# Order of the expert passes, time of the routing ranks, and order of the products in a streaming-encoder kernel

## The reference

```python
def swiglu(x, w1, w3, w2):
    return (jax.nn.silu(x @ w1) * (x @ w3)) @ w2

def moe_swiglu(h, router_w, w1, w3, w2):
    logits = (xf @ router_w).astype(jnp.float32)
    top_val, top_idx = lax.top_k(logits, TOP_K)
    gates = jax.nn.softmax(top_val, axis=-1)
    ...
    y = lax.map(expert_block, (buf_tok.reshape(n_blocks, EXPERT_BLOCK), block_exp))
    y = y.reshape(P, D) * buf_g[:, None].astype(y.dtype)
    out = jax.ops.segment_sum(y, buf_tok, num_segments=N + 1)[:N]
```

## Time and profile before

| | |
|---|---|
| median of 3 runs | 1400.2 us (1400.18 to 1401.83) |
| profiled execution, its own time | 1399.86 us |
| its span | 1398.1 us |
| TensorE busy | 1295.9 us (93%), mean granted clock 0.956 |
| VectorE busy | 920.8 us (66%) |
| ScalarE busy | 743.0 us (53%) |
| HBM read | 472.46 MB, 339 GB/s over the span |

### The profile page before, as it was taken

The page is one execution under the profiler, slowest core; times in us unless marked ns, Lnnn a source line. Parts: engine busy times, 40 slices in busy tenths (PEclk is TensorE's granted clock), DMA queues, the critical chain, the costliest instruction groups (busy, mean ns, idle before and its releaser), DMA issues. The chain is left out here.

```text
span 1398.1 us, 20800 instructions
## 1 busy us (share of the span) xinstructions
PE 1295.9 (93%) x7888; PEld 942.5 (67%) x7888; DVE 920.8 (66%) x1547; ACT 743.0 (53%) x1279; POOL 10.5 (1%) x45
## 2 busy tenths in 40 slices
PE   7999999999999999999779999999869997699985
PEld 5875899999888988786138888887216652067420
DVE  3788898887885669996049999998017730077201
ACT  4656554444563669893049998996016730067100
POOL 0000000000000200000000000000000000000000
PEclk9999999999999999999979999999969999799896
DMA  8986668879665449899999999999999979999796
GB/s 322 378 299 235 247 243 297 320 268 358 242 235 188 156 158 378 338 366 354 420 413 415 404 413 413 407 417 356 419 418 411 420 277 420 418 405 419 266 418 256
DMA packets 130146, 474.92 MB, mean 340 GB/s; under 512 B 9437, under 2 KB 11626, under 8 KB 107514
## 3 DMA queue, kind: packets, MB, share of 16 engines
q1 hardware_dynamic: 128672, 472.28, 87.0%
q10 hardware_dynamic: 1370, 1.25, 0.3%
HBM read 472.46 MB, written 1.05 MB: 339 GB/s over the span
## 5 line engine op out<-in xcount | busy, mean ns | idle before, releaser
L2315 ACT ACTIVATE hi_first<-ring 128x512 fp32r<-128x512 f32 x166 | 103.3, 632 | 43.0 <-DMA ring<-in_moe_w 30.1
L3139 DVE TENSOR_TENSOR lo_first<-ring,hi_first 128x512 fp32r<-128x512 f32 x166 | 108.7, 691 | 15.6 <-ACT hi_first L2315 15.3
L3139 DVE TENSOR_TENSOR lo_third<-ring,hi_third 128x512 fp32r<-128x512 f32 x168 | 109.9, 691 | 12.8 <-ACT hi_third L2315 12.0
L2315 ACT ACTIVATE hi_third<-ring 128x512 fp32r<-128x512 f32 x168 | 103.9, 632 | 19.4 <-PE bank L1748 12.8
L2315 ACT ACTIVATE hi_second<-ring 128x512 fp32r<-128x512 f32 x166 | 103.0, 633 | 18.9 <-PE bank L1748 12.9
L3139 DVE TENSOR_TENSOR lo_second<-ring,hi_second 128x512 fp32r<-128x512 f32 x166 | 108.6, 691 | 4.9 <-ACT hi_second L2315 4.3
L2556 DVE SCALAR_TENSOR_TENSOR ada_acc<-ring,c_act,ada_acc 128x512 f32<-128x512 f32 x140 | 105.1, 751 | 3.9
L1827 PE MATMUL bank<-ring,work 128*32 128x512 f32 x344 | 67.8, 874 | 37.3 <-DMA ring<-in_moe_w 37.3
L1833 PE MATMUL bank<-ring,work 128*32 128x512 f32 x672 | 90.1, 605 | 7.2 <-DMA ring<-in_moe_w 7.2
L1282 PE MATMUL bank<-hg_hi,w_hi 128*128 128x256 f32 x336 | 95.5, 284 | 0.4 <-DVE w_lo L2791 0.4
L1284 PE MATMUL bank<-hg_hi,w_lo 128*128 128x256 f32 x336 | 95.1, 283 | 0.0
(11 more groups left out here) (560 smaller groups left out, 3336.0 us busy)
## 6 DMA issues: line engine op xcount, KB each, us to landing
ring<-in_moe_w SPq DMA_DIRECT2D x216, 1024.0 KB, 18.6
ring<-in_ada_w SPq DMA_DIRECT2D x24, 2048.0 KB, 12.1
ring<-in_moe_w SPq DMA_DIRECT2D x48, 768.0 KB, 11.2
ring<-in_ffn_w SPq DMA_DIRECT2D x15, 2048.0 KB, 9.4
beside_x<-in_moe_w SPq DMA_DIRECT2D x18, 1024.0 KB, 17.7
beside_out<-in_moe_w SPq DMA_DIRECT2D x18, 1024.0 KB, 17.6
beside_w<-in_moe_w SPq DMA_DIRECT2D x18, 1024.0 KB, 17.0
beside_lo<-in_moe_w SPq DMA_DIRECT2D x18, 1024.0 KB, 19.6
```

Source lines behind the costliest of these rows:

```text
L2315: A(hi_piece(Q), raw_piece(SPLITS[r], q, j), ACT.Copy).then_inc(hi_done, 1)
L3139: v.tensor_tensor(lo_piece(Q), raw_piece(SPLITS[r], q, j), hi_piece(Q).bitcast(F32), ALU.subtract).then_inc(lo_done, 1)
```

## The change

The order becomes A head, B, A tail, C head, B, C tail, A head, B, A tail, A, B. Three light passes lie inside the first, the wide and the next ordinary pass; the wide pass is second. Each of these light passes has its own gather, in the head of its host at pieces 35 and 38. In a hosting ordinary pass `slots_turned` moves from piece 20 to 54. In the first pass the ranks move from piece 28 to 4 (the fifth piece), the gain vector from 36 to 12 and to banks 2 and 3, the tokens' places from 33 to 14, the light pass's table to 20, and the next passes' tables stay at 60. SP waits for the ranks after slot 11. The low-part product of each part comes last, in the dense stage and in the expert passes, and the wait for the low part stands before it; the other two products wait for the high part alone. Branches for overflow passes go six deep instead of four. Waits on earlier results are left out where there is no earlier result.

```diff
-BASE = "ABAABCBB"
+BASE = "ABCBABAB"
-PLACES = (NE - 1, 3, 1, 2, 4, 0, 5, 6)
+PLACES = (NE - 1, 3, 0, 4, 1, 5, 2, 6)
-MIDS = {5: 6}
+MIDS = {0: 1, 2: 3, 4: 5}
...
-    PT_AT = {"A": g_last["w3", 0] + 5, "C": g_last["w3", 2] + 5}
+    PT_AT = {"A": g_last["w3", 0] + 5, "host": PPC * CUT + 6, "C": g_last["w3", 2] + 5}
...
-    GAIN_AT = g_last["w3", 1] + 5
-    PLACES_AT = GAIN_AT - 8
-    OVER_AT = GAIN_AT + 12
-    DISPATCH_AT = {"A": OVER_AT + 12, "C": XPT_AT + 3}
+    PLACES_AT = 4
+    GATES_AT = 8
+    GAIN_AT = 12
+    TOKENS_AT = 14
+    MID_DISPATCH_AT = 20
+    DISPATCH_AT = {"A": g_last["w3", 1] + 29, "C": XPT_AT + 3}
...
-    GROUPS = [(0,), (1, 2), (3,), (4, 5), (6,), (7,)] + [(NE + o,) for o in range(OVER)]
-    group_in = {0: 1, 2: 2, 3: 3, 5: 5}
-    mid_group_in = {5: 4}
-    dispatched_in = {0: (1, 2), 2: (3,), 3: (4, 5, 6), 5: (7,)}
+    GROUPS = [(0,), (1,), (2,), (3,), (4,), (5,), (6,), (7,)] + [(NE + o,) for o in range(OVER)]
+    group_in = {0: 2, 2: 4, 4: 6, 6: 7}
+    mid_group_in = {0: 1, 2: 3, 4: 5}
+    dispatched_in = {0: (2, 3), 2: (4, 5), 4: (6,), 6: (7,)}
...
-                if m == 0 and i >= PER - NE + 1:
+                if m == 0 and (i == CUT - 1 or i >= PER - NE + 2):
                     j = len(ids)
                     sp.wait_ge(s_places, 1)
...
-                pe.wait_ge(lo_done, q + 1)
+                pe.wait_ge(hi_done, q + 1)
                 whi, wlo = split_tile(w_hi, q), split_tile(w_lo, q)
+                out = psum[4 + g % 2][:, o:o + S]
                 for k in range(KT):
-                    out = psum[4 + g % 2][:, o:o + S]
                     mm(out, whi[:, k, :], hg_hi[:, k, :], start=(k == 0), stop=False)
                     mm(out, whi[:, k, :], hg_lo[:, k, :], start=False, stop=False)
+                pe.wait_ge(lo_done, q + 1)
+                for k in range(KT):
                     last = mm(out, wlo[:, k, :], hg_hi[:, k, :], start=False, stop=(k == KT - 1))
...
-                    pe.wait_ge(lo_done, piece_no(m, q, 0) + 1)
...
-                        pe.wait_ge(lo_done, Q + 1)
+                        pe.wait_ge(hi_done, Q + 1)
...
                         mm(out[:, :], xhi, whi, start=first, stop=False)
-                        mm(out[:, :], xhi, wlo, start=False, stop=False)
-                        mm(out[:, :], xlo, whi, start=False, stop=end).then_inc(w_free, 1)
+                        mm(out[:, :], xlo, whi, start=False, stop=False)
+                        pe.wait_ge(lo_done, Q + 1)
+                        mm(out[:, :], xhi, wlo, start=False, stop=end).then_inc(w_free, 1)
...
-                    if q == PT_AT[kind]:
+                    if q == PT_AT[role(m)]:
                         slots_turned(m)
...
-                            last = mm(psum[6 + k // 4][:, (k % 4) * P:(k % 4 + 1) * P], ones[:], diag[:, k, :],
+                            last = mm(psum[2 + k // 4][:, (k % 4) * P:(k % 4 + 1) * P], ones[:], diag[:, k, :],
...
-                    if q == 8 and m == 0:
+                    if q == GATES_AT and m == 0:
                         first_gates()
...
-                    if q == PLACES_AT + 5 and m == 0:
+                    if q == TOKENS_AT and m == 0:
                         places_of_tokens()
+                    if q == MID_DISPATCH_AT and m == 0:
+                        dispatch(MIDS[m])
...
                         with pe.If(more[3] == 2):
                             overflow(3)
+                            with pe.If(more[4] == 2):
+                                overflow(4)
+                                with pe.If(more[5] == 2):
+                                    overflow(5)
```

More of the change, by code:

```diff
@@ L287, in build @@
         plan = sb("plan", [P, 2, NE])
-        with ExitStack() as of_ranks:
-            ranks_of = of_ranks.enter_context(nc.sbuf_tensor("ranks_of", [P, TT, NE * NE], F32))
+        ranks_of = sb("ranks_of", [P, TT, NE * NE])
         members_of, earlier_e = [ranks_of[:, tt, :] for tt in range(TT)]
-        mid_places = sb("mid_places", [P, TT, HALF], F32R)
+        mid_places = sb("mid_places", [P, TT, XT], F32R)
         rt = sb("rt", [P, 12, TT * NE])
@@ L303, in build @@
         h_hi = sb("h_hi", [P, TT, D], F32R)
-        Pm = sb("Pm", [P, TT, P + 2 * XT], F32R)
+        Pm = sb("Pm", [P, TT, P + XT], F32R)
         QK_FILLS = (0, 2, 1, 3, 4, 6, 5, 7)
@@ L686, in outs_before, with role @@
             return turn_no(m) - (m in MIDS) if m < NE else m - 1
+        def role(m):
+            return "host" if m in MIDS and KINDS[m] == "A" else KINDS[m]
         def down_bank(m):
@@ L1324, in ffn_out @@
                         mm(out, whi[:, 0, ms], xlo, start=False, stop=False, skip_group_check=True)
+                    pe.wait_ge(lo_done, q + 1)
+                    for m in range(KT):
+                        out = psum[m // 2][:, (m % 2) * S:(m % 2 + 1) * S]
+                        ms = slice(m * P, (m + 1) * P)
                         last = mm(out, wlo[:, 0, ms], xhi, start=False, stop=end, skip_group_check=True)
@@ L1708, in expert @@
                             pe.wait_ge(s_ea, chunk_no(m, c))
-                            if kind == "A" and c == 1:
+                            if kind == "A" and c == (2 if role(m) == "host" else 1):
                                 pe.wait_ge(s_gge, turn_no(m) + 1)
@@ L1714, in expert @@
                                 pe.wait_ge(s_scb, 4 * out_no(MIDS[m]) + 2)
-                            if c == 2 and m == 0:
+                        else:
+                            if c == 0 and m == 0:
                                 pe.wait_ge(s_g2e, 1)
-                        else:
-                            if c == 0 and m:
+                            if c == 0 and outs_before(m):
                                 pe.wait_ge(s_scb, 4 * outs_before(m))
@@ L1761, in expert @@
                             pe.wait_ge(s_hdl, chunk_no(m, turn))
-                        elif m:
+                        elif outs_before(m):
                             pe.wait_ge(s_scb, 4 * outs_before(m))
@@ L1811, in light @@
                         else:
-                            pe.wait_ge(s_scb, 4 * outs_before(m))
+                            if outs_before(m):
+                                pe.wait_ge(s_scb, 4 * outs_before(m))
                             pe.wait_ge(s_hdh, chunk_no(m, 0) + 1)
@@ L2426, in expert @@
                             A(hidx[:, turn % 2, 0:js, :], turned[:, :, 0:2 * XT], ACT.Silu).then_inc(s_xs, 1)
-                    if q == PT_AT[kind] + 1:
+                    if q == PT_AT[role(m)] + 1:
                         take_slots(m)
@@ L2435, in expert @@
                         for g in range(2):
-                            last = A(g2bc[:, g * 512:(g + 1) * 512], psum[6 + g][:, :], ACT.Copy)
+                            last = A(g2bc[:, g * 512:(g + 1) * 512], psum[2 + g][:, :], ACT.Copy)
                         last.then_inc(s_g2e, 1)
@@ L2502, in _ @@
                             overflow(3)
+                            with act.If(more[4] == 2):
+                                overflow(4)
+                                with act.If(more[5] == 2):
+                                    overflow(5)
             store_end()
@@ L3208, in take_spread @@
                 dst = x_acc[:, tt, half * 512:(half + 1) * 512]
-                if n == 0 and m:
+                if n == 0 and out_no(m):
                     dve.wait_ge(s_scb, 4 * out_no(m))
@@ L3354, in _ @@
                             overflow(3)
+                            with dve.If(more[4] == 2):
+                                overflow(4)
+                                with dve.If(more[5] == 2):
+                                    overflow(5)
 INPUTS = ["x", "c", "ada_w", "ada_b", "norm1_g", "norm2_g", "da_w_in", "da_q_gain", "da_k_gain", "da_lam_q1",
```

9 lines of the change are left out of this document (4 added, 5 removed).

## The result

The changed kernel takes 1409.0 us (median of 5 runs, 1406.9 to 1410.5) against 1400.2 us (5 runs). The ratio is 1.0061, 95% interval 1.0049 to 1.0074: slower by 8.5 us (0.61% of 1400.2; the two medians are 8.8 us apart). The forecast was 1409.5. The profiled execution took 1409.0 us with a span of 1407.2.

The account below looks back on a forecast made before the run. The prediction took the weight stream to bound the expert part, with joint computing stretches outrunning what the ring allows. Its terms summed to +9.8 us, 1409.7, stated as 1409.5 us, range 1394 to 1420.

Parts of the forecast that it names:

- The cause: Expert part: weight stream limits; joint stretches compute past data plus ring, 157.4 and 156.1 us against 148.2 allowed.
- The sum: Whole run: computing stretches and light passes added up, +9.8 us, giving 1409.7, stated as 1409.5 us.
- Low-part product last: Dense stage and expert passes: gain where a pass restarts behind a light one, 0.5 us in all, no more than 2.
- the dense stage's 0.4 us: Dense stage: all that VectorE's low parts cost TensorE there, 0.4 us.
- The seam behind the wide pass: Wide tail and third head: light gather 3.9, wide result's eight products 1.8, VectorE's longer first reads 0.4; 156.1 us together.
- five parts of lead: First pass, piece 28: VectorE is five parts ahead of TensorE's need for low parts and so hides the ranks.
- The ring's allowance: Between light passes: the stream idles when n slots' computing exceeds 5.11 n + 40.9 us, the ring's eight slots.
- the 3.6 us (1.6 + 2): Last stretch, where the stream sets the time: 1.6 us for the last half slot's products, 2 for a seam.
- Ranks, gather, last light pass: First head: early ranks 0.8 us, light gather 3.9, ending at 593.3; last light pass 72 to 76 us.
- the 3 to 6 that I gave as a sign: First head: a sign of being right was its ending 3 to 6 us later than 589.3, relative to its start.
- The rival of TensorE's step: All products: the 226.7 ns step falls to at most 213.3 ns, saving 17 us, so 1392; chance 6%.

Follow-up runs that it names:

- o_first: Changed kernel with the light pass put back out of the first pass, between it and the wide one, and overflow branches four deep: 1400.2 us.
- o_mid: Changed kernel with the wide pass third and a light pass still inside the first, two overflow passes fewer prepared: 1399.9 us.
- first_only: Changed kernel returned to the order of before, except one light pass inside the first; early ranks and low-part product last kept: 1404.7 us.
- u_low: Changed kernel with the old order of products and old waits, in the dense stage and expert passes: 1417.2 us.
- b_spread: Kernel before with a hosted result spread behind the fourth slot of a light pass instead of the second: 1393.9 us.

## Why the prediction was right, and what in it was not

*The cause* holds in the main. Three changes of the order (o_first, o_mid, first_only) came out within 2 us of sums of computing stretches and light passes, with opposite signs. Computing taken out of the wide head counts, 14.7 of 14.7 us, and the 3.8 us taken out of the last pass do not. How much of the loss comes of the longer stretches and how much of the work that each light pass inside another adds is open; both are terms of the sum, and the order runs change them together.

*The sum* hit by luck, because two errors of the same size cancel. **Low-part product last** was put at 0.5 us and no more than 2; it is worth 8.2 us in the changed kernel and 3.8 in the one before. The failing step was to read TensorE's rows in a steady stretch alone and to take the dense stage's 0.4 us for the whole kernel; the waits of the kernel before, shown under u_low, had 7.9 us in three waits for `lo_first`. Without it the order costs 17 us (u_low), not the 10.3 of my steps. The 7 us that were missing stand in u_low's stretches: first tail 63.8 against 61.4, wide tail and third head 78.6 + 81.1 = 159.7 against 156.1, and the three light passes in hosts 74.5, 80.6 and 75.0 against 73.7, 79.3 and 73.7: 2.4 + 3.6 + 3.4 = 9.4, less 2.0 by which the wide head (94.7) and the end (12.4) came out shorter than said. That makes 7.4 us in the profiled execution; the medians have 7.0.

*The seam behind the wide pass* was the largest single piece. I priced the ordinary pass behind it at 2.2 us more for the wide result. In the changed kernel the third head takes 80.3 us against 77.0 (70.9 + 3.9 + 1.8 + 0.4). TensorE there, and VectorE:

```profile
983.49 1.06 PE L1686 MATMUL bank<-ring,work 128*32 128x512 f32 x8
...
985.35 0.51 PE L1756 MATMUL bank<-hi_first,tokens_hi 128*128 128x512 f32 x1
...
992.62 0.39 PE L1757 MATMUL bank<-hi_third,tokens_lo 128*128 128x512 f32 x1
994.54 0.50 PE L1759 MATMUL bank<-lo_third,tokens_hi 128*128 128x512 f32 x1 [1.53 <-DVE lo_third L3160]
```

```profile
985.48 1.29 DVE L3208 TENSOR_TENSOR work<-bank,work 128x512 f32<-128x512 f32 x2 [1.15 <-PE bank L1686]
...
990.61 1.29 DVE L3160 TENSOR_TENSOR lo_second<-ring,hi_second 128x512 fp32r<-128x512 f32 x2 [0.61 <-ACT hi_second L2332]
991.82 1.41 DVE L3219 SCALAR_TENSOR_TENSOR hid_lo<-work,gcol,hid_hi 128x512 fp32r<-128x512 f32 x2
993.14 0.74 DVE L3222 SCALAR_TENSOR_TENSOR hid_lo<-work,gcol,hid_hi 128x512 fp32r<-128x512 f32 x1
993.81 1.28 DVE L3160 TENSOR_TENSOR lo_third<-ring,hi_third 128x512 fp32r<-128x512 f32 x2
```

Two things make up the 3.3 us. The wide pass's last 16 light products (L1686) stand behind its last low part, so that they fall into this stretch: 983.49 to 985.35, 1.9 us, which I had not counted for this pass. And TensorE waits 1.53 us for `lo_third`. In front of that low part VectorE does the wide result's three low halves, 1.41 + 0.74 us. I had let them hide behind five parts of lead; here VectorE has no such lead, since it had to wait for the wide pass's last products (1.15 us) and then scale the result. In o_mid the same wait is 1.5 us. With the 16 products (1.9) and the wide result's eight (1.8) that is 5.2 of the 7.4 us by which its ordinary pass is longer; the rest is open.

*The ring's allowance* of 40.9 us was too generous (34.4 or less). The prediction's own figures said so: a light pass whose data take 104.9 us took 73.7 behind a full ring, which is 31.2 less, or 34.8 with the 3.6 us (1.6 + 2) that the sum puts behind the stream. The sum did not use it where it decided, since I added computing and light passes there, but the sentence that no stretch of before goes over by itself is wrong: the 252.2 us of its two ordinary passes are past the limit of 214.6 + 34, and its wide head, 98.0 against 61.3 + 34, is over.

*Ranks, gather, last light pass* came as priced: nothing that can be told from zero for the ranks, a first head that ends 0.7 us earlier than said, and a last light pass of 74.1 instead of 85.7. (Counted from its own start the first head is 74.0 us against 71.4, so 2.6 longer, a little under the 3 to 6 that I gave as a sign.)

*The rival of TensorE's step* falls. Products are 227 ns apart in both orders, so the figure of the Trainium skill (TensorE: Matmul & The Clock Gate, Back-to-back issue gap) that stood beside it, 215.8 ns, is reached in neither.

## What to carry to other kernels

Where passes that compute slower than their weights arrive alternate with passes that are faster, cut the run into stretches between the fast ones and hold each stretch's computing against its data plus what the ring can really take. Moving a fast pass earlier lengthens the stretch behind it, and what it saves in front is paid there. Putting it inside a slow pass also adds work (10.2 us of computing in first_only), which shows unless the stream sets that stretch. A steady stretch of the trace tells nothing of the waits at a pass's edges: price a change of waits from the view of waits over the whole span.

## What was not expected of the hardware

In the kernel before a wait of 3.4 us on TensorE stands ahead of 16 products that take 9.1 us; without the wait they take 5.3. The two stretches, first before and then b_spread:

```profile
1310.40:1319.60 9.20, 9.12 (x16) 3.92 (x16) 2.09 (x4) 0.00 (x0) 0.00 (x0) 0.51 0.84 350
```

```profile
1311.80:1317.10 5.30, 5.30 (x20) 2.37 (x16) 2.09 (x4) 0.60 (x1) 0.00 (x0) 1.00 1.01 424
```

The granted clock is 0.51 (1.2 GHz) in the one and full in the other. The products' 3.8 us are more than half of the 6.5 us that b_spread gains (1393.9 against 1400.4 in the runs beside it), so the slower clock behind the wait costs about as much as the wait of 3.4 us itself. A restart behind a light pass runs in part at 1.2 GHz in every kernel here: for some 3 to 8 of its first 12 us the granted clock is 0.5 (the first tail's mean is 0.94). It may be that a wait less is worth more there than its own length, as the estimate under u_low has it; no run tries it alone.
